# Two attentions interleaved anew, and w_hi ahead of w_lo in the 512-column ups of a two-block transformer kernel

## Chip, cores and metric

One core of one Trainium2 chip. The metric is the device time of one execution in microseconds; less is better.

## What is computed

256 tokens of width 1024 pass through two transformer blocks, all weights in float32 from HBM. First block: gated MLP mixer, convolutional FFN, **differential attention** (8 heads, two softmax maps a head, their difference times v, an RMS norm a head), the same FFN again. Second block: pooling mixer, squared-ReLU MLP, **stick-breaking attention** (16 heads; weights from log-sigmoids and reversed cumulative sums), the same MLP again. Each sublayer is `h = h + rmsnorm(sublayer(rmsnorm(h)))`.

```python
p = jax.nn.softmax(s, axis=-1); attn = p[0] - lam_full * p[1]      # differential attention
o = rmsnorm(einsum('bhqk,bhkd->bhqd', attn, v), sub_g) * (1.0 - lambda_init)
excl = lax.cumsum(log1m, axis=3, reverse=True) - log1m             # stick-breaking attention
a = jnp.where(mask, jnp.exp(jax.nn.log_sigmoid(z) + excl), 0.0)
```

## The kernel before

**Precision by splitting.** Every float32 operand is split into a rounded high part and a low remainder; a product is hi x hi + hi x lo + lo x hi, three fp32r matmuls (`three`, L592).

**Units.** The weights come as 181 units of 128 x 2048 (1 MB). For each unit SyncE loads `raw` (3 buffers; the load of u waits for w_lo of u-3, L462), ScalarE rounds it into `w_hi` (4 buffers, `split_hi`, L279), VectorE subtracts it into `w_lo` (3 buffers, `split_lo`, L288) and TensorE uses both. `unit_done` of u - 4 frees w_hi, that of u - 3 frees w_lo. Each engine's order is written out by hand, with semaphores between them; ScalarE and VectorE do their splits at fixed places among their other work (`CUT = 3` units ahead of TensorE).

**Ups of FFN and MLP** (`unit_pair`, L611): the moving operand holds the high and low half of all 256 tokens side by side. Per k-tile and output tile one matmul with w_hi over 512 columns, then one with w_lo over 256. The first three ups of a phase (`first_ups`, L677) are cut by token halves instead: `half_pair` and `low_pair` of 16 matmuls with 256 columns each.

**Downs** (`unit_down`, L720, `last_downs`, L732): 24 matmuls of 512 columns a unit, 12 a token half. At the end of FFN and MLP the last three downs run half 0 of all, then half 1; the transposes of half 0 of the next input (`turn_half`, L755) stand ahead of the last half down. Behind the attentions the last two downs do so, and the transposes follow at the end (`by_threes` is false there, L353).

**Junctions** (L1126, L1458): result -> squares (ScalarE) -> gain and residual (VectorE) -> squares -> normed input -> transposes (TensorE) -> high part (ScalarE) -> low part (VectorE), a token half at a time. `n` counts junctions: J_DIFF and J_STICK stand behind the attentions.

**Differential attention** (TensorE L941 to L957, ScalarE L1335, VectorE L1758, POOL L531). Twelve projection units, q, k, v for each of four rounds of two heads (q and k: `unit_feat`; v: `unit_token`; 48 matmuls of 256 columns each), then four downs. A round: q of j, transposes and outputs of the heads of j-1 (`diff_turn`, `diff_av`), k, transposes back of the normed heads (`diff_back`), v, scores of j. Between them ScalarE does exponentials, copies and squares; POOL makes 1/rms of four (head, token half) pairs in five small operations (L538 to L546); VectorE scales (`diff_norm`) and splits (`diff_o_lo`). Scores of head h wait for o_lo of head h-2 (L860), whose PSUM bank they take.

**Stick-breaking attention** (L1069 to L1095): ten steps (`stick_step`: scores of t, cumulative sums of t-1, outputs of t-2), placed behind certain projection units (`STICK_AT`, L77).

**POOL** runs its list in order: after the differential attention it loads gains once the second half of the next input is there (L495), builds the band matrices of the pooling mixer (L553 to L580), and only then multiplies gate and up of the second FFN (L582, `gate_up`, L329).

## Time and profile before

| | us |
|---|---|
| median of 3 runs (lowest, highest) | 1113.28 (1112.42, 1113.76) |
| the profiled execution | 1113.68 |
| its span, first to last instruction | 1111.7 |
| TensorE busy in the span | 1076.2 |
| VectorE, ScalarE, POOL busy | 756.8, 634.1, 129.1 |

Mean granted TensorE clock 0.994. Busy times are unions of the intervals in which an instruction ran. A matmul's own duration holds its way through the array, so that the distance of two starts, and not the duration, says how fast they follow each other. A row's "idle before" is the time since the engine's previous instruction ended, with what ended it.

### The profile page before, as it was taken

The numbers are of one execution on the slowest core, as the hardware profiler recorded it, in microseconds if no ns is written. First come the engines' busy times: TensorE is split into PE (matmuls) and PEld (weight loads), VectorE is DVE, ScalarE is ACT, GpSimd is POOL, SyncE is SP. The second block draws the span as 40 slices with busy tenths as digits, with TensorE's granted clock in tenths as the row PEclk, the third lists the DMA queues.
The fourth block names the chain that finished last, engine by engine and source line by source line (L and its number), as shares of the span: only waits on it lengthen the run. The fifth ranks groups of instructions, "written<-read, shape, count | busy, mean of one in ns | idle before, by whom it ended". The sixth has DMA issues, their size and how long they took to land.

```text
span 1111.7 us, 15698 instructions
## 1 busy us (share of the span) xinstructions
PE 1076.2 (97%) x6390; PEld 940.0 (85%) x6390; DVE 756.8 (68%) x883; ACT 634.1 (57%) x848; POOL 129.1 (12%) x131
## 2 busy tenths in 40 slices
PE   9999999999899988999998999999999998999997
PEld 8978888887899887888887888888899878888886
DVE  6878777667777677767668865656775657665654
ACT  6656755656655666755656544444577865453532
POOL 0001332120021155222110000000000000000000
PEclk9999999999999999999999999999999999999999
DMA  9836775454544365555552655555364234646451
GB/s 340 318 115 230 243 246 198 180 190 152 190 136 157 126 227 170 190 190 194 185 188 83 227 195 198 181 198 183 120 228 142 97 108 166 209 171 208 170 189 38
DMA packets 31142, 202.21 MB, mean 182 GB/s; under 512 B 3640, under 2 KB 3808, under 8 KB 8544
## 3 DMA queue, kind: packets, MB, share of 16 engines
q1 hardware_dynamic: 28032, 189.16, 48.3%
q0 software_dynamic: 3040, 12.07, 3.4%
q8 instruction: 50, 0.82, 0.3%
q14 instruction: 20, 0.16, 0.0%
HBM read 200.15 MB, written 2.63 MB: 182 GB/s over the span
## 4 chain that ended last, share of the span: by engine, by line
PE 75%; DVE 12%; ACT 5%; POOL 4%; issue 4%; DMA 0%; SPq 0%; DVEq 0%; ACTq 0%; POOLq 0%
PE wk L620 20%; PE wk L622 10%; PE acc L594 9%; PE acc L596 8%; PE acc L595 8%; PE wk L594 3%; PE wk L596 3%; PE wk L595 3%; DVE w_lo L295 3%; PE wk L643 2%; PE wk L652 2%; ACT w_hi L286 2%; DVE x L1477 1%; DVE region L1685 1%; PE acc L643 1%
## 5 line engine op out<-in xcount | busy, mean ns | idle before, releaser
L295 DVE TENSOR_TENSOR w_lo<-raw,w_hi 128x2048 fp32r<-128x2048 f32 x168 | 384.6, 2293 | 74.4 <-ACT w_hi L286 66.6
L620 PE MATMUL wk<-a_hl,w_hi 128*128 128x512 f32 x1024 | 363.7, 399 | 3.4 <-DVE region L1675 3.2
L286 ACT ACTIVATE w_hi<-raw 128x2048 fp32r<-128x2048 f32 x173 | 329.3, 1906 | 6.9 <-DMA raw<-ws 6.2
L622 PE MATMUL wk<-a_hl,w_lo 128*128 128x256 f32 x1024 | 287.3, 281 | 0.0
L620 PEld LDWEIGHTS wk<-a_hl,w_hi 128*128 128x128 f32 x1024 | 192.4, 188 | 51.9 <-DVE region L1675 5.0
L622 PEld LDWEIGHTS wk<-a_hl,w_lo 128*128 128x128 f32 x1024 | 193.3, 189 | 1.5
L594 PE MATMUL acc<-w_hi,b_hl 128*128 128x512 f32 x432 | 169.4, 392 | 1.3 <-DVE w_lo L295 1.3
L595 PE MATMUL acc<-w_lo,b_hl 128*128 128x512 f32 x432 | 168.5, 390 | 0.0
L596 PE MATMUL acc<-w_hi,b_hl 128*128 128x512 f32 x432 | 168.4, 390 | 0.0
L1368 ACT ACTIVATE region<-wk 128x512 f32<-128x512 f32 x30 | 17.9, 597 | 163.9 <-PE wk L622 156.7
L594 PEld LDWEIGHTS acc<-w_hi,b_hl 128*128 128x128 f32 x432 | 81.1, 188 | 19.5 <-DVE w_lo L295 2.1
L596 PEld LDWEIGHTS acc<-w_hi,b_hl 128*128 128x128 f32 x432 | 81.1, 188 | 17.7
L595 PEld LDWEIGHTS acc<-w_lo,b_hl 128*128 128x128 f32 x432 | 81.1, 188 | 15.4
L1685 DVE SCALAR_TENSOR_TENSOR region<-region,prm 128x256 f32<-128x256 f32 x176 | 78.8, 489 | 19.4 <-ACT region L1280 17.8
L1792 DVE TENSOR_TENSOR region<-wk,region 128x512 f32<-128x512 f32 x30 | 20.7, 691 | 94.3 <-ACT region L1368 94.3
L1270 ACT ACTIVATE region<-wk 128x512 f32<-128x512 f32 x42 | 24.9, 592 | 80.0 <-PE wk L622 76.3
L336 POOL TENSOR_TENSOR region<-region 128x512 f32<-128x512 f32 x20 | 49.5, 2474 | 178.4 <-ACT region L1287 178.4
L498 POOL DMA_DIRECT2D gain<-gains x13 | 7.3, 563 | 458.5 <-DVE region L1493 448.7
L594 PE MATMUL wk<-a_hl,w_hi 128*128 128x256 f32 x208 | 59.7, 287 | 0.2 <-DVE w_lo L295 0.2
L596 PE MATMUL wk<-a_hl,w_lo 128*128 128x256 f32 x208 | 58.9, 283 | 0.0
L595 PE MATMUL wk<-a_hl,w_hi 128*128 128x256 f32 x208 | 58.8, 283 | 0.0
L1675 DVE TENSOR_TENSOR region<-wk,region 128x512 f32<-128x512 f32 x42 | 28.8, 687 | 39.8 <-ACT region L1270 39.7
(256 smaller groups left out, 1658.2 us busy)
## 6 DMA issues: line engine op xcount, KB each, us to landing
raw<-ws SPq DMA_DIRECT2D x173, 1024.0 KB, 4.9
gain<-gains POOLq DMA_DIRECT2D x13, 512.0 KB, 5.0
raw<-ws SPq DMA_DIRECT2D x8, 256.0 KB, 6.6
region<-rows SPq DMA_DIRECT2D x1, 1664.0 KB, 9.6
lines_dram<-line_dram POOLq DMA_DIRECT2D x1, 1536.0 KB, 8.3
bias<-gains POOLq DMA_DIRECT2D x3, 512.0 KB, 7.0
region<-xT SPq DMA_DIRECT2D x4, 256.0 KB, 5.0
x<-x_rows SPq DMA_DIRECT2D x1, 1024.0 KB, 7.2
```

Of the source, the lines that this page charges most:

```text
L286: act.activation(w_hi[:, u % HIGH, :], raw[:, u % RAW, :], ACT.Copy).then_inc(hi_ready, 1)
L295: dve.tensor_tensor(w_lo[:, u % LOW, :], raw[:, u % RAW, :], w_hi[:, u % HIGH, :].bitcast(F32), ALU.subtract).then_inc(lo_ready, 1)
L336: eng.tensor_tensor(hf[:, p:p + 2, :], gl[:, p:p + 2, :], cv[:, p:p + 2, 1, :], ALU.mult)\
L594: pe.matmul(o, still, moving, start=first, stop=False, skip_group_check=True)
L595: pe.matmul(o, still, moving_lo, start=False, stop=False, skip_group_check=True)
L596: return pe.matmul(o, still_lo, moving, start=False, stop=last, skip_group_check=True)
L620: pe.matmul(banks[:, m, :], wh[:, k, c], a_hl[:, k, :, :].rearrange("p e t -> p (e t)"), start=k == 0, stop=False, skip_group_check=True)
L622: mm = pe.matmul(banks[:, m, T:2 * T], wl[:, k, c], a_hi[:, k, :], start=False, stop=k == DT - 1, skip_group_check=True)
L643: pe.matmul(banks[:, m, :].rearrange("p (e t) -> p e t", e=2)[:, :, c], wh[:, k, m * P:(m + 1) * P], x[:, k, :, c], start=h == 0 and k == ...
L1270: act.activation(ffn_low[:, a, :, :], ffn_banks(n, i, a)[:, :, T:2 * T], ACT.Copy).then_inc(s["low"], 1)
L1675: dve.tensor_tensor(hb[:, p + a, :, 2:HW], ffn_banks(n, i, a)[:, :, 0:T], ffn_low[:, a, :, :], ALU.add)\
L1685: dve.scalar_tensor_tensor(out=cv[:, p + a, q, :], in0=hb[:, p + a, q, tap:tap + T], scalar=prm[:, bass.ds(col, 1)], in1=cv[:, p + a, q, : ...
```

## The change

- `unit_pair` runs its 16 w_hi matmuls first, waiting for w_hi alone, and then the 16 w_lo ones (`low_pair`).
- `feat_part` and `token_part` are `unit_feat` and `unit_token` in pieces: over some k-tiles, and for v over one token half. Both attentions place scores, transposes and outputs inside units.
- Differential attention: in round 0 head 0's scores stand ahead of v's low part, head 1's in the middle of q of round 1. From round 1 on: q, transposes of both heads, 2 k-tiles of k, outputs, the rest of k, half the k-tiles of v's token half 0, transposes back, the other half, scores, v's token half 1. Mean and eps move from POOL to VectorE (`diff_rms`); POOL does the power alone.
- Stick-breaking attention: units in the order q0 q1 k0 v0 k1 v1 q2 ..., steps in the middle of units; `stick_step` of VectorE is cut in two, with a split between.
- The four downs of both attentions run by token halves (`down_tokens`), and the transposes stand ahead of the last half down. For that the last w_lo has a buffer of its own (`SPARE`).
- In both junctions ScalarE and VectorE have the order of the FFN junctions.

The diff, cut to its core ("..." where lines are left out, indentation reduced):

```diff
+STICK_UNITS = (("q", 0), ("q", 1), ("k", 0), ("v", 0), ("k", 1), ("v", 1), ("q", 2), ("k", 2), ("v", 2), ("q", 3),
+       ("k", 3), ("v", 3))
+STICK_MID = {3: 0, 4: 1, 5: 2, 6: 3, 8: 4, 9: 5, 11: 6}
+STICK_END = {11: 7}
...
+SPARE = {U_DIFF + 15: o_lo_t[:, :, :].rearrange("p k t -> p (k t)"),
+         U_STICK + 15: b_hl[:, 0:DT // 2, :, :].rearrange("p k e t -> p (k e t)")}
+def low_of(u):
+    return SPARE[u] if u in SPARE else w_lo[:, u % LOW, :]
...
+    if u == U_STICK + 15:
+        dve.wait_ge(unit_done, U_STICK + 12)
+    elif u >= LOW and u not in SPARE:
         dve.wait_ge(unit_done, u - LOW + 1)
...
 def by_threes(n):
-    return n not in (J_DIFF, J_POOL, J_STICK)
+    return n != J_POOL
...
-        over = rden[:, :, :].rearrange("p e (n m) -> p e n m", m=2)[:, :, :, 0]
-        four = lambda t: t[:, c].rearrange("p (e n) -> p e n", e=2)
-        pool.tensor_tensor(four(o_ms), four(o_ss), over, ALU.mult).then_inc(o_mean, 1)
-        pool.wait_ge(o_mean, 4 * j + 1)
-        pool.tensor_tensor(four(o_ms), four(o_ms), over, ALU.mult).then_inc(o_mean, 1)
-        pool.wait_ge(o_mean, 4 * j + 2)
-        pool.tensor_scalar(o_ms[:, c], o_ms[:, c], 1.0 / P, EPS, ALU.mult, ALU.add).then_inc(o_mean, 1)
-        pool.wait_ge(o_mean, 4 * j + 3)
-        pool.tensor_tensor(o_rs[:, c], o_ms[:, c], minus_half[:, :], ALU.pow).then_inc(o_mean, 1)
-        pool.wait_ge(o_mean, 4 * j + 4)
-        pool.tensor_tensor(four(o_rs), four(o_rs), over, ALU.mult).then_inc(o_rms, 1)
+        pool.wait_ge(o_mean, 2 * j + 2)
+        pool.tensor_tensor(o_rs[:, c], o_ms[:, c], minus_half[:, :], ALU.pow).then_inc(o_rms, 1)
...
     def unit_pair(u, banks):
-        pe.wait_ge(lo_ready, u + 1)
+        pe.wait_ge(hi_ready, u + 1)
         wh = w_hi[:, u % HIGH, :].rearrange("p (k m) -> p k m", k=DT)
-        wl = w_lo[:, u % LOW, :].rearrange("p (k m) -> p k m", k=DT)
         for k in range(DT):
             for m in range(2):
-                c = slice(m * P, (m + 1) * P)
-                pe.matmul(banks[:, m, :], wh[:, k, c], a_hl[:, k, :, :].rearrange("p e t -> p (e t)"),
+                pe.matmul(banks[:, m, :], wh[:, k, m * P:(m + 1) * P], a_hl[:, k, :, :].rearrange("p e t -> p (e t)"),
                           start=k == 0, stop=False, skip_group_check=True)
-                mm = pe.matmul(banks[:, m, T:2 * T], wl[:, k, c], a_hi[:, k, :],
-                               start=False, stop=k == DT - 1, skip_group_check=True)
-        mm.then_inc(unit_done, 1)
+        low_pair(u, banks)
...
+    def feat_part(u, bank, ks, hi=a_hi, lo=a_lo):
+        if ks[0] == 0:
+            pe.wait_ge(lo_ready, u + 1)
+        wh = w_hi[:, u % HIGH, :].rearrange("p (k m) -> p k m", k=DT)
+        wl = w_lo[:, u % LOW, :].rearrange("p (k m) -> p k m", k=DT)
+        for k in ks:
+            for m in range(2):
+                c = slice(m * P, (m + 1) * P)
+                mm = three(wk[:, bank, m * T:(m + 1) * T], wh[:, k, c], wl[:, k, c],
+                           hi[:, k, :], lo[:, k, :], k == 0 and m == 0, k == DT - 1)
+        if ks[-1] == DT - 1:
+            mm.then_inc(unit_done, 1)
+    def token_part(u, bank, h, ks, hi, lo):
+        if h == 0 and ks[0] == 0:
+            pe.wait_ge(lo_ready, u + 1)
+        c = slice(h * P, (h + 1) * P)
+        wh = w_hi[:, u % HIGH, :].rearrange("p (k m) -> p k m", k=DT)
+        wl = w_lo[:, u % LOW, :].rearrange("p (k m) -> p k m", k=DT)
+        for k in ks:
+            mm = three(wk[:, bank, h * T:(h + 1) * T], hi[:, k, c], lo[:, k, c], wh[:, k, :], wl[:, k, :],
+                       k == 0 and h == 0, k == DT - 1)
+        if h and ks[-1] == DT - 1:
+            mm.then_inc(unit_done, 1)
...
+    def down_tokens(n, u, h, pair, res, first=False):
+        last = u == LAST[n]
+        if h == 0:
+            pe.wait_ge(lo_ready, u + 1)
+        for f in range(2):
+            for kk in range(2):
+                mm = down_half(u, h, kk, f, *pair, res, first and kk == 0, last and kk == 1)
+            if last:
+                mm.then_inc(unit_done if h and f else res_done, 1)
+        if h and not last:
+            mm.then_inc(unit_done, 1)
...
+    def diff_first(base):
+        half_pair(base, wk[:, 0:2, :], J_FFN0, 0)
+        half_pair(base + 1, wk[:, 2:4, :], J_FFN0, 0)
+        turn_half(J_FFN0, 1)
+        half_token(base + 2, acc[:, 3, :], J_FFN0, 0, a_hi, a_lo)
+        half_pair(base, wk[:, 0:2, :], J_FFN0, 1)
+        low_pair(base, wk[:, 0:2, :])
+        half_pair(base + 1, wk[:, 2:4, :], J_FFN0, 1)
+        low_pair(base + 1, wk[:, 2:4, :])
+        half_token(base + 2, acc[:, 3, :], J_FFN0, 1, a_hi, a_lo)
+        pe.wait_ge(dq_ready, 1)
+        pe.wait_ge(dk_ready, 1)
+        diff_scores(0)
+        low_token(base + 2, acc[:, 3, :], a_hi)
+        feat_part(base + 3, 0, range(0, 4))
+        pe.wait_ge(dv_ready, 2)
+        diff_scores(1)
+        feat_part(base + 3, 0, range(4, DT))
+    diff_first(U_DIFF)
     for j in range(1, 4):
-        projections(U_DIFF, j, 0, dreleased)
-        outputs_pair(j - 1)
-        projections(U_DIFF, j, 1, dreleased)
+        u = U_DIFF + 3 * j
+        if j > 1:
+            pe.wait_ge(dq_ready, j)
+            feat_part(u, 0, range(DT))
+        pe.wait_ge(dk_ready, j)
+        if j > 1:
+            pe.wait_ge(dv_ready, 2 * j)
+            diff_turn(2 * j - 2)
+            diff_turn(2 * j - 1)
+            feat_part(u + 1, 1, range(0, 2))
+            diff_av(2 * j - 2)
+            diff_av(2 * j - 1)
+            feat_part(u + 1, 1, range(2, DT))
+        else:
+            diff_turn(0)
+            feat_part(u + 1, 1, range(0, 4))
+            diff_av(0)
+            diff_turn(1)
+            feat_part(u + 1, 1, range(4, 6))
+            diff_av(1)
+            feat_part(u + 1, 1, range(6, DT))
+        pe.wait_ge(dv_ready, 2 * j)
+        token_part(u + 2, 2, 0, range(0, 4), a_hi, a_lo)
         diff_back(j - 1)
-        projections(U_DIFF, j, 2, dreleased)
-        scores_pair(j)
-    pe.wait_ge(dv_ready, 8)
-    unit_down(U_DIFF + 12, *b_pair(0), True, res=wk)
+        token_part(u + 2, 2, 0, range(4, DT), a_hi, a_lo)
+        pe.wait_ge(dq_ready, j + 1)
+        pe.wait_ge(dk_ready, j + 1)
+        diff_scores(2 * j)
+        diff_scores(2 * j + 1)
+        token_part(u + 2, 2, 1, range(DT), a_hi, a_lo)
+    u = U_DIFF + 12
+    down_tokens(J_DIFF, u, 0, b_pair(0), wk, True)
+    down_tokens(J_DIFF, u + 1, 0, b_pair(1), wk)
     outputs_pair(3)
-    unit_down(U_DIFF + 13, *b_pair(1), False, res=wk)
+    down_tokens(J_DIFF, u + 2, 0, b_pair(2), wk)
     diff_back(3)
-    last_downs(J_DIFF, U_DIFF + 14, (b_pair(2), b_pair(3)), (None, (o_lo, 8)), res=wk)
+    down_tokens(J_DIFF, u, 1, b_pair(0), wk, True)
+    pe.wait_ge(o_lo, 8)
+    down_tokens(J_DIFF, u + 3, 0, b_pair(3), wk)
+    down_tokens(J_DIFF, u + 1, 1, b_pair(1), wk)
+    down_tokens(J_DIFF, u + 2, 1, b_pair(2), wk)
+    turn_half(J_DIFF, 0)
+    down_tokens(J_DIFF, u + 3, 1, b_pair(3), wk)
     ffn_phase(1, U_FFN1, J_DIFF)
...
+        q0, q1, k0 = wk[:, 0:2, :], wk[:, 2:4, :], acc[:, 2:4, :]
+        turn_half_kv(0)
+        half_pair(base, q0, J_MLP0, 0)
+        half_pair(base + 1, q1, J_MLP0, 0)
+        pe.wait_ge(blo_ready, 2)
+        turn_half(J_MLP0, 1)
+        half_pair(base + 2, k0, J_MLP0, 0, b_hl, True)
+        half_pair(base, q0, J_MLP0, 1)
+        turn_half_kv(1)
+        low_pair(base, q0)
+        half_pair(base + 1, q1, J_MLP0, 1)
+        low_pair(base + 1, q1)
+        half_pair(base + 2, k0, J_MLP0, 1, b_hl, True)
+        low_pair(base + 2, k0, b_hi)
...
+    for c in range(3, 12):
+        if c == 3:
+            pe.wait_ge(sq_ready, 2)
+        stick_unit(c, 0)
+        if c in STICK_MID:
+            stick_there(STICK_MID[c])
+            stick_step(STICK_MID[c])
+        stick_unit(c, 1)
+        if c in STICK_END:
+            stick_there(STICK_END[c])
+            stick_step(STICK_END[c])
...
+    u = U_STICK + 12
+    pe.wait_ge(so_lo, 2)
+    down_tokens(J_STICK, u, 0, o_pair(0), wk, True)
+    pe.wait_ge(so_lo, 4)
+    down_tokens(J_STICK, u + 1, 0, o_pair(1), wk)
     pe.wait_ge(sv_ready, 8)
-    pe.wait_ge(so_lo, 2)
-    unit_down(U_STICK + 12, *o_pair(0), True, res=wk, last_bank=(so_lo, 6))
     stick_step(8)
-    unit_down(U_STICK + 13, *o_pair(1), False, res=wk)
+    pe.wait_ge(so_lo, 6)
+    down_tokens(J_STICK, u + 2, 0, o_pair(2), wk)
     stick_step(9)
-    last_downs(J_STICK, U_STICK + 14, (o_pair(2), o_pair(3)), (None, (so_lo, 8)), res=wk)
+    down_tokens(J_STICK, u, 1, o_pair(0), wk, True)
+    pe.wait_ge(so_lo, 8)
+    down_tokens(J_STICK, u + 3, 0, o_pair(3), wk)
+    down_tokens(J_STICK, u + 1, 1, o_pair(1), wk)
+    down_tokens(J_STICK, u + 2, 1, o_pair(2), wk)
+    turn_half(J_STICK, 0)
+    down_tokens(J_STICK, u + 3, 1, o_pair(3), wk)
...
-        if by_threes(n):
-            input_hi(0)
+        if n == J_MLP0:
+            split_hi(act, last + 3)
+        input_hi(0)
         result_squares(1)
-        if not by_threes(n):
-            input_hi(0)
...
-    for j in range(4):
+    low_copy(U_DIFF, wk[:, 0:2, :], diff_low[:, 0, :, :], d_low)
+    split_hi(act, U_DIFF + 3)
+    low_copy(U_DIFF + 1, wk[:, 2:4, :], diff_low[:, 1, :, :], d_low)
+    split_hi(act, U_DIFF + 4)
+    token_copy(U_DIFF + 2, 0, 3, av, ACT.Copy, dv_ready, src=acc)
+    diff_exp(0)
+    diff_exp(1)
+    diff_probs(0)
+    split_hi(act, U_DIFF + 5)
+    diff_probs(1)
+    diff_squares(0)
+    diff_squares(1)
+    for j in range(1, 4):
         u = U_DIFF + 3 * j
-        if j:
+        if j > 1:
             diff_outputs(j - 1)
-        else:
-            low_copies(u, diff_low, d_low)
         split_hi(act, u + CUT)
-        if j:
-            diff_o_hi(j - 1)
         split_hi(act, u + 1 + CUT)
-        token_copy(u + 2, j, 2 if j else 3, av, ACT.Copy, dv_ready, src=wk if j else acc)
-        split_hi(act, u + 2 + CUT)
+        diff_o_hi(j - 1)
         diff_exp(2 * j)
         diff_exp(2 * j + 1)
+        token_copy(u + 2, j, 2, av, ACT.Copy, dv_ready)
+        split_hi(act, u + 2 + CUT)
...
+    low_copy(U_STICK + 1, wk[:, 2:4, :], stick_low[:, 1, :, :], s_low)
+    act.wait_ge(sq_ready, 1)
+    low_copy(U_STICK + 2, acc[:, 2:4, :], stick_low[:, 0, :, :], s_low)
+    split_hi(act, U_STICK + 4)
+    split_hi(act, U_STICK + 5)
+    for c in range(3, 12):
+        kind, j = STICK_UNITS[c]
+        if c in STICK_MID:
+            stick_step(STICK_MID[c])
+        split_hi(act, U_STICK + c + CUT)
+        if kind == "v":
+            token_copy(U_STICK + c, j, 2, av, ACT.Copy, sv_ready)
+        if c in STICK_END:
+            stick_step(STICK_END[c])
+    split_hi(act, U_STICK + 15)
     stick_step(8)
-    split_hi(act, U_STICK + 12 + CUT)
...
-        if by_threes(n):
-            lo_half(dve, last + 1, 0)
+        lo_half(dve, last + 1, 0)
...
-            lo_half(dve, last + 1, 1)
-            input_lo(0)
+        lo_half(dve, last + 1, 1)
+        input_lo(0)
...
+    def diff_rms(j):
+        c = slice(4 * j, 4 * j + 4)
+        under = den[:, :, :].rearrange("p e (n m) -> p e n m", m=2)[:, :, :, 0]
+        four = lambda t: t[:, c].rearrange("p (e n) -> p e n", e=2)
+        dve.scalar_tensor_tensor(out=four(o_rs), in0=under, scalar=EPS, in1=under, op0=ALU.mult, op1=ALU.mult)                   .then_inc(o_mean, 1)
+        dve.wait_ge(o_mean, 2 * j + 1)
+        dve.wait_ge(o_squared, 4 * (j + 1))
+        dve.scalar_tensor_tensor(out=four(o_ms), in0=four(o_ss), scalar=1.0 / P, in1=four(o_rs), op0=ALU.mult,
+                                 op1=ALU.add).then_inc(o_mean, 1)
...
-    for j in range(4):
+    feat_sum(wk[:, 0:2, :], diff_low[:, 0, :, :], d_low, 1, qT[:, 0:2, :], dq_ready)
+    split_lo(dve, U_DIFF + 3)
+    feat_sum(wk[:, 2:4, :], diff_low[:, 1, :, :], d_low, 2, kT[:, 0:2, :], dk_ready)
+    diff_bias(0)
+    split_lo(dve, U_DIFF + 4)
+    diff_combine(0)
+    diff_bias(1)
+    diff_combine(1)
+    split_lo(dve, U_DIFF + 5)
+    for j in range(1, 4):
         u = U_DIFF + 3 * j
-        if j == 0:
-            feat_sum(u, 0, diff_low, d_low, qT[:, 0:2, :], dq_ready)
-            feat_sum(u + 1, 1, diff_low, d_low, kT[:, 0:2, :], dk_ready)
-        else:
-            feat_copy(u, 0, qT[:, 2 * j:2 * j + 2, :], dq_ready)
-        split_lo(dve, u + CUT)
-        if j:
-            diff_norm(j - 1)
-            feat_copy(u + 1, 1, kT[:, 2 * j:2 * j + 2, :], dk_ready)
-            diff_o_lo(j - 1)
-        split_lo(dve, u + 1 + CUT)
+        feat_copy(u, 0, qT[:, 2 * j:2 * j + 2, :], dq_ready)
+        if j == 1:
+            split_lo(dve, u + CUT)
+        diff_rms(j - 1)
+        diff_norm(j - 1)
+        if j > 1:
+            split_lo(dve, u + CUT)
+        feat_copy(u + 1, 1, kT[:, 2 * j:2 * j + 2, :], dk_ready)
+        if j > 1:
+            split_lo(dve, u + 1 + CUT)
+        diff_o_lo(j - 1)
         for part in (diff_bias, diff_combine):
             part(2 * j)
             part(2 * j + 1)
+        if j == 1:
+            split_lo(dve, u + 1 + CUT)
         split_lo(dve, u + 2 + CUT)
+    diff_rms(3)
+    diff_norm(3)
     split_lo(dve, U_DIFF + 12 + CUT)
-    diff_norm(3)
     diff_o_lo(3)
-    split_lo(dve, U_DIFF + 13 + CUT)
     junction(J_DIFF)
...
+    feat_sum(wk[:, 0:2, :], stick_low[:, 0, :, :], s_low, 1, qT[:, 0:2, :], sq_ready)
+    split_lo(dve, U_STICK + 3)
+    feat_sum(wk[:, 2:4, :], stick_low[:, 1, :, :], s_low, 2, qT[:, 2:4, :], sq_ready)
+    feat_sum(acc[:, 2:4, :], stick_low[:, 0, :, :], s_low, 3, kT[:, 0:2, :], sk_ready)
+    for c in range(3, 12):
+        kind, j = STICK_UNITS[c]
         u = U_STICK + c
-        if c == 0:
-            feat_sum(u, 0, stick_low, s_low, qT[:, 0:2, :], sq_ready)
-            feat_sum(u + 1, 1, stick_low, s_low, kT[:, 0:2, :], sk_ready)
-        elif kind == 0:
+        if c in STICK_MID:
+            stick_weights(STICK_MID[c])
+        if c == 3:
+            split_lo(dve, U_STICK + 4)
+        split_lo(dve, u - 1 + CUT)
+        if kind == "q":
             feat_copy(u, 0, qT[:, 2 * j:2 * j + 2, :], sq_ready)
-        elif kind == 1 and j:
+        elif kind == "k":
             feat_copy(u, 1, kT[:, 2 * j:2 * j + 2, :], sk_ready)
-        if c in STICK_AT:
-            stick_step(STICK_AT[c], split=u + CUT)
-        else:
-            split_lo(dve, u + CUT)
-    stick_step(8)
+        if c in STICK_MID:
+            stick_rest(STICK_MID[c])
+    stick_weights(7)
+    split_lo(dve, U_STICK + 11 + CUT)
+    stick_rest(7)
+    stick_weights(8)
+    stick_rest(8)
     split_lo(dve, U_STICK + 12 + CUT)
-    stick_step(9)
-    split_lo(dve, U_STICK + 13 + CUT)
+    stick_weights(9)
```

## Rows read from the trace of the kernel before

**Rows 1.** The profile page of the kernel before, parts 1 and 4.
```profile
PE 1076.2 (97%) x6390; PEld 940.0 (85%) x6390; DVE 756.8 (68%) x883; ACT 634.1 (57%) x848; POOL 129.1 (12%) x131
...
PE 75%; DVE 12%; ACT 5%; POOL 4%; issue 4%; DMA 0%; SPq 0%; DVEq 0%; ACTq 0%; POOLq 0%
```

**Rows 2.** Waits of TensorE: total us, times, longest us.
```profile
PE wk L643 <- DVE a_hl L1500: 7.3, 2, 3.7
...
PE acc L875 <- DVE region L1732: 3.4, 4, 1.4
...
PE acc L863 <- ACT region L1207: 1.0, 1, 1.0
```

**Rows 3.** The page's group of the 512-column ups, and its timeline over one unit.
```profile
L620 PE MATMUL wk<-a_hl,w_hi 128*128 128x512 f32 x1024 | 363.7, 399 | 3.4 <-DVE region L1675 3.2
...
461.44 0.40 PE L620 MATMUL wk<-a_hl,w_hi 128*128 128x512 f32 x1
...
467.09 0.40 PE L594 MATMUL acc<-w_hi,b_hl 128*128 128x512 f32 x1
```

**Rows 4.** Timeline of a run of 512-column and of one of 256-column matmuls.
```profile
450.29 0.40 PE L594 MATMUL acc<-w_hi,b_hl 128*128 128x512 f32 x1
...
451.47 0.39 PE L596 MATMUL acc<-w_hi,b_hl 128*128 128x512 f32 x1
...
455.80 0.39 PE L620 MATMUL wk<-a_hl,w_hi 128*128 128x512 f32 x1
...
621.00 2.08 PE L652 MATMUL wk<-a_hl,w_lo 128*128 128x256 f32 x16
622.92 2.08 PE L643 MATMUL wk<-a_hl,w_hi 128*128 128x256 f32 x16
```

**Rows 5.** Windows: from:to, length, busy us (count) of each engine, PEclk, DMA share, GB/s.
```profile
274.94:280.19 5.25, 4.00 (x33) 3.78 (x31) 3.61 (x9) 3.70 (x9) 0.00 (x0) 1.00 0.38 158
393.15:403.80 10.65, 6.83 (x42) 6.26 (x42) 6.55 (x14) 6.93 (x14) 2.55 (x5) 0.84 0.10 33
920.32:930.67 10.35, 6.67 (x41) 6.22 (x41) 6.28 (x13) 6.66 (x14) 0.53 (x1) 0.84 0.11 34
...
925.20:928.61 3.41, 3.30 (x15) 3.33 (x16) 2.20 (x5) 2.21 (x4) 0.46 (x1) 0.50 0.00 0
...
814.52:920.32 105.80, 104.71 (x755) 93.43 (x753) 63.59 (x62) 80.72 (x91) 0.00 (x0) 1.00 0.40 140
```

**Rows 6.** One round of the first attention: its window, then rows of the timeline.
```profile
319.74:342.52 22.78, 22.14 (x184) 21.28 (x183) 16.38 (x27) 12.97 (x33) 3.79 (x5) 1.00 0.41 140
...
328.25 0.55 PE L875 MATMUL acc<-ident,region 128*128 128x128 f32 x3 [0.56 <-DVE region L1732]
...
329.93 0.39 PE L887 MATMUL acc<-region 128*128 128x128 f32 x2
...
330.87 1.92 ACT L286 ACTIVATE w_hi<-raw 128x2048 fp32r<-128x2048 f32 x1
331.06 0.20 POOL L538 TENSOR_TENSOR o_ms<-o_ss,region 128x4 f32<-128x4 f32 x1 [18.65 <-ACT region L1318]
...
331.90 1.01 POOL L544 TENSOR_TENSOR o_rs<-o_ms,minus_half 128x4 f32<-128x4 f32 x1
332.81 2.29 DVE L295 TENSOR_TENSOR w_lo<-raw,w_hi 128x2048 fp32r<-128x2048 f32 x1 [1.81 <-ACT w_hi L286]
```

**Rows 7.** Timeline: the norm of round 1, and the transposes that wait for it.
```profile
312.44 1.13 DVE L1741 TENSOR_SCALAR region<-acc,o_rs 128x128 f32<-128x128 f32 x4
...
313.15 0.91 PE L896 MATMUL acc<-ident,region 128*128 128x128 f32 x4
```

**Rows 8.** The chain of waits after the first attention: start us, us, what.
```profile
400.96 0.29 issue
...
426.64 1.26 POOL region L336
...
438.89 0.50 PE wk L620
```

167 lines of the change are left out of this document (60 added, 107 removed).

## The prediction

> **What bounds the kernel now.** I read the page first. TensorE is busy 97% of the span and makes 75% of the chain that ends last [rows 1]; VectorE and ScalarE stand at 68% and 57%. So only two things can move the time: how closely TensorE's matmuls follow one another, and the 35 us in which it stands idle, or runs at half clock. The view of its waits [rows 2] says where it idles: 7.3 us in two pauses of up to 3.7 us at the junctions behind the two attentions, 3.4 us in the first attention (transposes of the probabilities wait for VectorE), 1.0 us there at the first scores; and 3.2 us at the 512-column ups [rows 3], at the start of the second FFN. Then I went into these places one by one.
>
> **Part 1: the order inside a 512-column up.** Before, each w_hi matmul (512 columns) is followed by its w_lo one (256 columns). One unit of 16 such pairs starts at 461.44 and is over at 467.09: 5.65 us [rows 3]. The page counts 1024 pairs, thus 64 units. The change runs 16 w_hi, then 16 w_lo. What the two kinds cost in runs of their own is in [rows 4]: 24 matmuls of 512 columns take 450.29 to 455.80; its first 5 take 1.18 us (0.236 each), the other 19 take 4.33 (0.228 each). 16 matmuls of 256 columns take 622.92 - 621.00 = 1.92 us. If the wide run is slow at its start each time, a unit costs 1.18 + 11 x 0.228 + 1.92 = 5.61; if it isn't, 16 x 0.228 + 1.92 = 5.57. That is 0.04 to 0.08 us a unit, 2.6 to 5.1 us over 64. I take **4.0**, between, since the rows show a slow start behind alternating matmuls and none behind a run of narrow ones. About 0.3 is lost where TensorE waits for others afterwards (second FFN's start). So **-3.7**. The wait for w_lo moves behind the w_hi run; no row of TensorE in these lines waits for w_lo, so that gives nothing. The bound against me: a wide run that stays at 0.236 and w_lo as now gives 5.70, +3 us over 64.
>
> By the Trainium skill ("TensorE: Matmul & The Clock Gate", Back-to-back issue gap) the distance of two matmuls follows from the column count alone, so that an order of the same matmuls would be worth 0. The trace does not agree fully: the pair takes 0.353 alternating, 0.348 in runs.
>
> **Part 2: junctions behind the attentions.** Today the last two downs alone are run by token halves, and the transposes of half 0 come after all downs. In the first FFN's junction, whose order the attentions are now given (transposes of half 0 before the last down's half 1), TensorE reaches the transposes of half 1 5.25 us after the last down, at full clock; in the attentions' junctions it takes 10.65 and 10.35 us, with a mean clock of 0.84 [rows 5]. The clock fell to 0.50 (1.2 GHz) for 3.41 us just when TensorE resumed from its pause [rows 5]; half of that, 1.7 us, is lost. The 1.4 us pause of the first FFN's junction had no such fall. After the change the way is 1.3 us (8 transposes, now ahead of the last half down) + 0.3 us (their wait) + 5.25 = 6.9. For the second attention: 10.35 - 6.9 = **-3.4**. Nothing behind it waits for something else: TensorE has no wait in the last MLP. Bounds: -1.7 (the clock still falls) to -4.
>
> **Part 3: the second attention's body.** Same matmuls, eight steps of scores, sums and outputs as before, put inside value and query projections in place of between them. In this stretch TensorE has work for 104.7 of 105.8 us and ScalarE, the next, for 80.7 [rows 5], so a step's chain on ScalarE and VectorE is covered, in either order. About 1 us of TensorE's idle time there may go, and I count as much anew (the first value unit waits for the second q sum; the last two cumulative sums wait for ScalarE, which gets a split between step 7 and step 8). **0**, bounds -1.5 to +2.
>
> **Part 4: the first attention's body.** One round takes 22.78 us now [rows 6], 48 x 3 projections' matmuls at 0.12 us making 17.3 of it. What goes: the scores' wait for ScalarE (1.0 idle) and the transposes' waits (3.4 idle, four of them) [rows 2]. These are idle times from one matmul's end to the next one's start; in starts, as the wait of [rows 6] at 328.25 shows (0.56 idle, 0.76 later than the two transposes' own distance), each costs 0.2 more: 1.0 + 3.4 + 5 x 0.2 = 5.4. The waits for the norm, too short for a row, are estimated at 0.2 to 0.3 each, together 0.9: about 6.3 us. POOL's chain of five small operations (331.06 to the norm at about 335.2) shrinks to the power alone (1.01).
>
> What comes: VectorE's order in round 1 is copy q, *split of unit 6*, then the mean, the power (POOL), the norm. That split needs ScalarE's w_hi of unit 6, which stands behind both heads' squares. From the last output matmul (329.93) to the squares' end (331.06) is 1.1 us; + ScalarE's split 1.9, VectorE's split 2.3 (its row waits for just this split of ScalarE now, 1.81 us), two small operations 0.4 (as L538, 0.20 each), the power 1.1, first norm to transposes 0.7 (312.44 to 313.15, [rows 7]) = 7.5 us. TensorE has as cover two k-tiles of the k unit (12 matmuls, 1.44) and a quarter of the v unit (12, 1.44). So it waits about 7.5 - 2.9 - 0.2 = **4.4 us**; now the whole k unit (5.8) covers 5.9.
> Rounds 2 and 3: scores of a round need o_lo, which VectorE does behind norm, split, copy and split: 1.1 + 0.4 + 1.1 + 1.1 + 2.3 + 0.7 + 2.3 + 0.5 = 9.5 us behind the last output matmul; TensorE's cover is 36 + 12 + 12 matmuls and the transposes, 7.2 + 0.7, and gaps: wait 1.2 each, **2.4**. The end (norm 3, o_lo 8, turn) 0.9. Four more changes between f32 and f32r matmuls and the short blocks, 0.2 each: 0.8. Sum: 4.4 + 2.4 + 0.9 + 0.8 - 6.3 = +2.2.
>
> The junction: half 1's normed input is there at 400.96 [rows 8], 7.8 us behind the last down (393.15). New: 1.6 + 5.25 + 0.7 = 7.5. That is -0.3. **All that counts here is this moment**, since POOL builds the bands only then: the chain of waits runs from 400.96 through POOL to 426.64 (its first gate of the FFN) and leaves it only near 438.89, where TensorE resumes [rows 8]. Whatever TensorE gains at this junction, its clock too, ends in a longer wait at 430 to 439. So +1.9 stays whole. A pause of 4.4 us is longer than the 3.7 us behind which the clock fell; the same fall costs up to 1.7, part of it may lie in the pause itself: I take 1.3; and 0.2 for one more fall at the longer wait in the FFN. First attention: **+3.4**, bounds -0.5 (VectorE's split finds its w_hi earlier than I count, no fall) to +6.
>
> The skill's same page (HAM oscillation) says that idle gaps bring the clock down to half; by it the fall behind the 4.4 us wait is sure, and the two falls at the junctions go. The trace agrees in that each pause of 3.7 us had one.
>
> **Sum.** -3.7 - 3.4 + 0 + 3.4 = **-3.7 us**. The profiled execution took 1113.68 (span 1111.7 and 2.0 around it), 0.4 above the median 1113.28; I put the change against the median: 1109.6.
>
> **Rivals.**
> A. *The first attention loses nothing* (the waits at the norm are covered, and the clock stays): -3.7 - 3.4 + 0 = 1106.2. For it: VectorE is busy only 16.4 of 22.8 us in a round, POOL's chain gets 3 us shorter. Against: the order of round 1 leaves 2.9 us of cover. 20%.
> B. *The order of the ups gives nothing*, as the rule above has it: 0 - 3.4 + 3.4 = 1113.3. For it: the slow start of the wide run. 13%.
> C. *The pause behind the second attention stays long enough for the clock to fall*: -3.7 - 1.7 + 3.4 = 1111.3. Against: the same order at the first FFN pauses 1.4 us. 10%.
> D. *Slower: wide runs never settle.* Each change from 256 to 512 columns shows 0.236 to 0.24 for five matmuls. If a run across two banks stays at 0.240, a unit costs 16 x 0.240 + 1.92 = 5.76, +0.11, and 64 units +7.0: 1113.3 + 7.0 = 1120.3. It passes into slower from a mean of 0.236 on (with parts 2 to 4 at 0, +0.03 us a unit = 2.2 us). Against: 19 of 24 run at 0.228, though in one bank's groups. 8%.
> My forecast has the rest, 49%.
>
> **Numbers.** 0.2% (2.2 us) is about what a measurement of this kernel can tell. The forecast with its bounds is faster in four of five of its cases; with A that makes 0.65 faster; B, C and the forecast's upper end 0.27 same; 0.08 slower. The range goes from 1105.0 (below A) to 1113.9 (above B), leaving out D and the tails.
>
> **What would show it.** L620's block of 16 in 3.65 to 3.75 us and L652's in 1.92; two falls of the clock fewer at the junctions, the transposes of half 1 5.25 us after the last down; a TensorE wait of 4 us or so for L1741's kind (norm) in round 1 with a fall of the clock right behind; o_lo ending waits of about 1 us ahead of the scores in rounds 2 and 3; POOL's bands starting 2 to 3.5 us later, and the waits at the second FFN's start longer than 3.2 us. I am wrong if the norm's wait in round 1 is under 2 us, if blocks of w_hi take 3.8 us or more, or if the second attention shows new waits of over 2 us in total.

## The result and the profile after

The changed kernel takes 1102.66 us (median of 4 runs, 1102.10 to 1103.36) beside 1113.50 for the kernel before in the same session: ratio 0.9904, 95% interval 0.9892 to 0.9915, so 10.8 us less. The forecast was 1109.6, its range 1105.0 to 1113.9: the direction was right, the gain almost three times what was forecast, and the time outside the range. The profiled execution took 1102.57, its span 1100.7 (before 1113.68 and 1111.7).

The page of the changed kernel, parts 1, 4 and 5:

```profile
PE 1066.9 (97%) x6390; PEld 939.1 (85%) x6390; DVE 757.6 (69%) x893; ACT 634.5 (58%) x849; POOL 115.8 (11%) x115
...
PE 77%; DVE 12%; issue 4%; ACT 4%; POOL 3%; DMA 1%; SPq 0%; DVEq 0%; ACTq 0%; POOLq 0%
...
L619 PE MATMUL wk<-a_hl,w_hi 128*128 128x512 f32 x1024 | 243.8, 390 | 4.5 <-DVE region L1781 4.4
```

The same matmuls, the same engine ahead. Its waits, from the view of TensorE's waits (total us, times, longest):

```profile
PE wk L619 <- DVE region L1781: 4.4, 4, 2.7
PE acc L921 <- DVE region L1859: 4.1, 1, 4.1
PE acc L888 <- DVE b_hl L1865: 2.2, 2, 1.1
```

The two pauses of 3.7 us of [rows 2] are gone, and so is the 3.4 us for VectorE in the first attention. New are a wait of 4.1 us for the norm (L921) and two for o_lo (L888), both forecast; and the ups at the second FFN's start wait 4.2 of these 4.4 us (the rest is in the first FFN), not 3.2.

To see where the 11.0 us of span went, I took marks that both traces have, mostly the start of `turn_half(n, 1)`, the transposes of half 1 at each junction:

| mark | before | after | shift | of this stage |
|---|---|---|---|---|
| GMLP's junction | 89.72 | 89.38 | -0.34 | -0.34 |
| first FFN's junction | 280.19 | 278.22 | -1.97 | -1.63 |
| last wait at the second FFN's start over | 438.89 | 436.85 | -2.04 | **-0.07** |
| second FFN's junction | 597.92 | 594.24 | -3.68 | -1.64 |
| first 512-column up of MLP 0 | 630.60 | 626.16 | -4.44 | **-0.76** |
| first MLP's junction | 799.07 | 793.12 | -5.95 | -1.51 |
| first 512-column up of MLP 1 | 944.98 | 935.32 | -9.66 | **-3.71** |
| end of the span | 1111.7 | 1100.7 | -11.0 | -1.34 |

The four rows of stages full of 512-column ups give 1.63 + 1.64 + 1.51 + 1.34 = 6.1. The second attention with its junction gives 3.7, the first attention 0.1, a junction that the change does not touch 0.8, and 0.3 was there before the first 512-column up (in the runs below the mark of the GMLP's junction lies between 89.05 and 90.14).

**The ups.** Timeline of the changed kernel over two units and the down behind them:

```profile
453.55 3.79 PE L619 MATMUL wk<-a_hl,w_hi 128*128 128x512 f32 x16
457.18 2.08 PE L649 MATMUL wk<-a_hl,w_lo 128*128 128x256 f32 x16
459.09 3.82 PE L619 MATMUL wk<-a_hl,w_hi 128*128 128x512 f32 x16
462.75 2.08 PE L649 MATMUL wk<-a_hl,w_lo 128*128 128x256 f32 x16
464.66 0.40 PE L595 MATMUL acc<-w_hi,b_hl 128*128 128x512 f32 x1
```

By the starts, 16 w_hi take 3.63 and 3.66, 16 w_lo 1.91. Two units take 11.11 us; the same two before:

```profile
472.59 0.39 PE L620 MATMUL wk<-a_hl,w_hi 128*128 128x512 f32 x1
...
483.88 0.40 PE L594 MATMUL acc<-w_hi,b_hl 128*128 128x512 f32 x1
...
472.59:489.38 16.79, 16.79 (x89) 1.00 0.54 188
```

11.29 us; with the down behind them 16.79 against 16.58 (453.55 to 470.13). So 0.09 us a unit, and the down takes 5.47 in place of 5.50, so 0.03 more. In the MLPs, one up and its down have a period of 11.01 (637.20 to 648.21) in place of 11.11 (641.76 to 652.87 before). That is 0.10 a unit with its share of the down in either phase, 6.4 over 64 units; a little of it is lost in the first ups of a phase.

**The junction behind the second attention.** Windows of the changed kernel, from the transposes of half 0 and from the end of the last down to the transposes of half 1:

```profile
911.60:920.74 9.14, 7.88 (x52) 6.96 (x52) 6.99 (x14) 6.28 (x14) 0.00 (x0) 1.00 0.35 115
915.49:920.74 5.25, 3.99 (x33) 3.78 (x31) 3.61 (x9) 3.70 (x9) 0.00 (x0) 1.00 0.38 158
```

The 5.25 us are those of [rows 5] to the hundredth, at full clock. The 0.31 us wait and the 1.07 us of transposes ahead of the last down make 6.63, where it was 10.35.

**The first attention.** Timeline of round 1, VectorE and TensorE:

```profile
309.61 2.29 DVE L308 TENSOR_TENSOR w_lo<-raw,w_hi 128x2048 fp32r<-128x2048 f32 x1 [2.58 <-ACT w_hi L297]
313.40 1.13 DVE L1859 TENSOR_SCALAR region<-acc,o_rs 128x128 f32<-128x128 f32 x4 [1.23 <-POOL o_rs L547]
314.06 1.21 PE L921 MATMUL acc<-ident,region 128*128 128x128 f32 x4 [4.08 <-DVE region L1859]
...
313.00:319.80 6.80, 5.74 (x28) 5.13 (x30) 3.01 (x8) 0.95 (x2) 0.36 (x1) 0.50 0.41 146
```

TensorE waits as forecast, and the clock is at 0.50 (1.2 GHz) for 6.8 us, 5.7 of them behind the wait, where I had priced a stretch of 3.4. And still this attention cost nothing in the end. The timeline of POOL, first of the kernel before, then of the changed one, has the reason (the last row of each is VectorE's, its three splits):

```profile
401.25 1.17 POOL L498 DMA_DIRECT2D gain<-gains  x2 [20.55 <-DVE region L1493]
405.55 8.62 POOL L563 TENSOR_SCALAR_AFFINE_SELECT region<-region 128x256 f32<-128x256 f32 x8
...
426.61 1.28 POOL L336 TENSOR_TENSOR region<-region 128x512 f32<-128x512 f32 x1
...
406.27 7.13 DVE L295 TENSOR_TENSOR w_lo<-raw,w_hi 128x2048 fp32r<-128x2048 f32 x3
```

```profile
401.58 1.12 POOL L511 DMA_DIRECT2D gain<-gains  x2 [22.86 <-DVE region L1603]
405.84 6.29 POOL L564 TENSOR_SCALAR_AFFINE_SELECT region<-region 128x256 f32<-128x256 f32 x8
...
424.57 1.29 POOL L349 TENSOR_TENSOR region<-region 128x512 f32<-128x512 f32 x1
...
403.27 6.88 DVE L308 TENSOR_TENSOR w_lo<-raw,w_hi 128x2048 fp32r<-128x2048 f32 x3
```

POOL starts 0.33 us later than before, 2.3 later against the first FFN's end, but its first gate comes 2.04 us earlier. Eight affine selects take 8.62 or 6.29 us: one takes 0.3 to 0.4 by itself and 2.2 to 2.4 where a split of VectorE runs beside it, and three met one before, two after. Shortest, median and longest of the eight in ns, before and changed:

```profile
L563 POOL TENSOR_SCALAR_AFFINE_SELECT region<-region x8: 293/403/2445, 405.5 to 413.9; 128x256 f32<-128x256 f32 x4, 128x128 f32<-128x128 f32 x4
L564 POOL TENSOR_SCALAR_AFFINE_SELECT region<-region x8: 288/394/2327, 405.8 to 411.8; 128x256 f32<-128x256 f32 x4, 128x128 f32<-128x128 f32 x4
```

The one fewer is the 2.3 us. By the Trainium skill ("SBUF — State Buffer", SBUF: two separate sides) VectorE and GpSimd share a port pair that whichever starts first holds for its whole instruction while the other is blocked, where both read SBUF and VectorE has two inputs there; the trace agrees: each of the five long affine selects ends 0.1 to 0.3 us behind the split beside it. VectorE's three splits stand behind the a_lo of half 1, thus behind TensorE's transposes of half 1, and these come 3.1 us earlier (403.80, 400.68).

### The profile page after: what moved, and what is told of

Same layout as the page of the kernel before. It is cut to its first block, busy times and chain, and to the rows that moved or that the text cites. A ratio compares the mean times of both kernels' runs of the same rounds, so it can differ in the third digit from the quotient of the medians.

```text
span 1100.7 us, 15695 instructions
## 1 busy us (share of the span) xinstructions
PE 1066.9 (97%) x6390; PEld 939.1 (85%) x6390; DVE 757.6 (69%) x893; ACT 634.5 (58%) x849; POOL 115.8 (11%) x115
## 4 chain that ended last, share of the span: by engine, by line
PE 77%; DVE 12%; issue 4%; ACT 4%; POOL 3%; DMA 1%; SPq 0%; DVEq 0%; ACTq 0%; POOLq 0%
PE wk L619 19%; PE wk L649 11%; PE acc L595 8%; PE acc L596 8%; PE acc L597 8%; PE wk L595 4%; PE wk L597 4%; PE wk L596 4%; DVE w_lo L308 4%; PE wk L640 1%; DVE x L1587 1%; DVE region L1603 1%; DVE region L1791 1%; DVE w_lo L319 1%; PE acc L640 1%
## 5 line engine op out<-in xcount | busy, mean ns | idle before, releaser
L308 DVE TENSOR_TENSOR w_lo<-raw,w_hi 128x2048 fp32r<-128x2048 f32 x164 | 375.0, 2290 | 60.8 <-ACT w_hi L297 53.6
L619 PE MATMUL wk<-a_hl,w_hi 128*128 128x512 f32 x1024 | 243.8, 390 | 4.5 <-DVE region L1781 4.4
L649 PEld LDWEIGHTS wk<-a_hl,w_lo 128*128 128x128 f32 x1216 | 155.1, 191 | 5.1
L649 PE MATMUL wk<-a_hl,w_lo 128*128 128x256 f32 x1216 | 158.0, 283 | 0.0
L595 PE MATMUL wk<-a_hl,w_hi 128*128 128x256 f32 x192 | 55.2, 288 | 0.0
L597 PE MATMUL wk<-a_hl,w_lo 128*128 128x256 f32 x192 | 54.3, 283 | 0.0
L596 PE MATMUL wk<-a_hl,w_hi 128*128 128x256 f32 x192 | 54.3, 283 | 0.0
```

What stands on the lines that cost most here:

```text
L308: dve.tensor_tensor(low_of(u), raw[:, u % RAW, :], w_hi[:, u % HIGH, :].bitcast(F32), ALU.subtract).then_inc(lo_ready, 1)
L595: pe.matmul(o, still, moving, start=first, stop=False, skip_group_check=True)
L596: pe.matmul(o, still, moving_lo, start=False, stop=False, skip_group_check=True)
L597: return pe.matmul(o, still_lo, moving, start=False, stop=last, skip_group_check=True)
L619: pe.matmul(banks[:, m, :], wh[:, k, m * P:(m + 1) * P], a_hl[:, k, :, :].rearrange("p e t -> p (e t)"), start=k == 0, stop=False, skip_gr ...
L649: mm = pe.matmul(banks[:, m, T:2 * T], wl[:, k, m * P:(m + 1) * P], hi[:, k, :], start=False, stop=k == DT - 1, skip_group_check=True)
```

## Experiments

Times of the runs are held against 1113.5 to 1113.8 for the kernel before, measured with each group of runs. Intervals are at 95%.

**1. The ups' order alone.** The kernel before, with

```diff
-                pe.wait_ge(lo_ready, u + 1)
+                pe.wait_ge(hi_ready, u + 1)
...
-                        mm = pe.matmul(banks[:, m, T:2 * T], wl[:, k, c], a_hi[:, k, :],
-                                       start=False, stop=k == DT - 1, skip_group_check=True)
-                mm.then_inc(unit_done, 1)
+                low_pair(u, banks)
```

> The kernel before with one part of the change alone: a 512-column up runs its 16 w_hi matmuls, then its 16 w_lo ones. Theory S (the units' closer spacing is the largest part of the gain; in the changed kernel's trace a unit takes 5.545 us where it took 5.65): 64 x 0.10 = 6.4 us, 0.3 to 1 of it lost where the second FFN's start waits for POOL's gate: -5.5 to -6.3 us, about 1107.5. Rival P (the prediction's own size, 0.04 to 0.08 us a unit): -2.3 to -4.8, about 1109.6. Rival N (the order alone gives nothing, the shift comes from the attentions): within 1 us of before. A fall of TensorE's clock at a junction that comes or goes is worth up to 1.7 us either way and is read in the granted clock.

1107.51 us, ratio 0.9948 (0.9934 to 0.9963): -6.2 us. Theory S holds, P and N fall. That alone is 1.7 times what the prediction gave the part. By the marks of its trace the four stages of ups give 6.0 of the 6.0 us of span. The rest cancels: the clock did not fall at the pooling junction (-0.8), but it stood at half for 6.8 us, not 3.4, behind the pause at the second attention (+0.7).

**2. Everything but the ups' order.** The changed kernel with the old `unit_pair`.

> The changed kernel with its 512-column ups alternating again, all else of the change kept. Theory S: the change less 6 us, so 4.5 to 5.3 us faster than before (about 1108.5). Rival P: the change less 4, so 6.5 to 7 us faster (1106.7). Rival N: as the changed kernel, 10.8 us faster (1102.7).

1109.96 us, ratio 0.9966 (0.9954 to 0.9977): -3.7 us, +7.3 on the changed kernel. That is beyond what S had named (-4.5 to -5.3), on the side away from P and N. What S left out is the pooling junction: here the clock fell behind it as before, in the changed kernel it did not (0.8 us, below). The four stages of ups take what they took before, to 0.14 us in all. This run prices the attentions without the ups. Its marks are 280.71 (+0.52 on before), 439.06 (+0.17) and, for the first 512-column up of MLP 1, 941.95 (-3.03), with 799.21 (+0.14) ahead: the first attention gives -0.35, the second -3.2. It shows the failed step in its plainest form, as nothing but the attentions differs from before:

```profile
403.83 1.12 POOL L511 DMA_DIRECT2D gain<-gains  x2 [22.86 <-DVE region L1607]
408.08 6.30 POOL L564 TENSOR_SCALAR_AFFINE_SELECT region<-region 128x256 f32<-128x256 f32 x8
...
426.78 1.28 POOL L349 TENSOR_TENSOR region<-region 128x512 f32<-128x512 f32 x1
```

POOL starts at 403.83, against 401.25: less the 0.52 this is 2.06 us later, close to the +1.9 that I had worked out. The gate comes at 426.78 against 426.61, 0.35 earlier by the same measure.

**3, 4. What in the order of the ups costs.** First groups of two (`for m in range(2)` around each kind), then strict alternation with each w_lo matmul one step later, so that its bank isn't that of the matmul ahead.

> The changed kernel with ups in groups of two w_hi and two w_lo matmuls: half as many changes between 512 and 256 columns as alternating, no wide run longer than two. Theory S1 (each change of width costs, 0.0065 us a pair of changes): half of the gain stays, 3 us slower than the changed kernel, 1105.8. Theory S2 (the first five wide matmuls behind a narrow one are slow, 0.236 in place of 0.227): nothing stays, 6 us slower, 1108.7. Theory S3 (what costs is that w_lo's result bank is that of the matmul just ahead, which groups of two avoid): all stays, 1102.7.

> The changed kernel with ups that alternate between 512 and 256 columns, but each w_lo matmul one w_hi matmul later than before, so that it never adds into the bank of the matmul just ahead of it. Theory S3 (what cost 0.1 us a unit was that bank): all of the gain stays, 1102.7 to 1103.5. Rival S4 (the alternation itself costs it): nothing stays, 6 to 7 us slower than the changed kernel, 1109.5.

Groups of two: 1103.50, ratio 0.9910 (0.9895 to 0.9924). Crossed alternation: 1109.18, ratio 0.9956 (0.9942 to 0.9970). The windows over two units and their down, of groups of two, then of the crossed order:

```profile
454.09:470.68 16.59, 16.59 (x90) 1.00 0.58 192
```

```profile
455.34:472.09 16.75, 16.75 (x90) 1.00 0.55 190
```

16.79 alternating, 16.75 crossed, 16.59 by twos, 16.58 in runs. Groups of two also keep the old wait for w_lo ahead of the unit, so that the moved wait is worth at most the 0.8 us by which they are slower than the changed kernel. The bank is worth little (S3 falls with the second run); a single narrow matmul between wide ones costs (S4), and two together are nearly as good as sixteen, which neither S1 nor S2 had. Why two suffice stays open.

**5. The wait for the norm in round 1.** The changed kernel with

```diff
-                if j == 1:
-                    split_lo(dve, u + CUT)
                 diff_rms(j - 1)
                 diff_norm(j - 1)
-                if j > 1:
-                    split_lo(dve, u + CUT)
+                split_lo(dve, u + CUT)
```

> The changed kernel with VectorE's order in round 1 of the first attention turned: mean, norm, and only then the split of unit 6, as in rounds 2 and 3. Theory W (the 4.2 us wait for the norm and the 5.8 us at half clock behind it, worth 2.9, are real time, and what is gained before the second FFN is kept): 4.0 + 2.9 less a new wait of about 1.5 us for o_lo ahead of the round's scores: 5.4 us faster than the changed kernel, 1097.3. Rival K (the start of the second FFN waits for POOL anyway, as the prediction's part 4 has it for what TensorE gains): under 1 us faster, 1102.

1098.87 us, ratio 0.9868 (0.9853 to 0.9883): 3.8 less than the changed kernel, where W had 5.4. The profiled execution took 1097.99 at a mean clock of 0.999, 4.6 less than the changed kernel's; two of the four took 1099.8 and 1099.9, at 0.996. TensorE's waits in the first attention are now

```profile
PE acc L888 <- DVE b_hl L1865: 3.6, 3, 1.4
PE acc L785 <- DVE region L1603: 1.4, 2, 1.3
```

The wait for the norm is gone, a third one for o_lo came (1.4), and in this execution the clock does not fall before the span's end. The transposes of half 1 behind this attention stand 117.50 us behind the first FFN's (122.46 in the changed kernel): 5.0 us. The last wait at the second FFN's start is over at 432.19, 4.66 earlier. So K falls: what TensorE gains here is kept.

**6. POOL started later.** The changed kernel with four more memsets ahead of the bands.

> The changed kernel with four more memsets (1.4 us with their wait) on POOL ahead of the bands. Theory V (POOL's progress there is pinned to the end of VectorE's three splits, beside which one of POOL's operations takes 2.2 us in place of 0.4; the 1.4 us are swallowed by the first of them): POOL's first gate and the time as in the changed kernel, 1102.7. Rival C (the chain runs from the normed input through POOL at fixed length, as the prediction's part 4 had it): gate and second FFN's start 1.4 us later, 1104.1.

1102.48 us, ratio 0.9900 (0.9886 to 0.9915). The timeline of POOL:

```profile
401.10 1.12 POOL L512 DMA_DIRECT2D gain<-gains  x2 [22.91 <-DVE region L1607]
...
405.35 1.50 POOL L560 MEMSET region<- 128x384 f32 x4
406.93 4.74 POOL L568 TENSOR_SCALAR_AFFINE_SELECT region<-region 128x256 f32<-128x256 f32 x8
...
424.11 1.28 POOL L350 TENSOR_TENSOR region<-region 128x512 f32<-128x512 f32 x1
```

From its start to its gate POOL takes 23.01 us; in the changed kernel, with 1.5 us less to do, 22.99. C, the prediction's reading, falls. V holds in that the time and the gate stay; what sets the length is how many of POOL's operations meet a split (one of the eight here, two in the changed kernel), not a fixed distance from the last split.

**7, 8. What removed the pause behind the second attention.** The changed kernel with `turn_half(J_STICK, 0)` one line further down, behind the last down's half 1; and the kernel before with the order of transposes alone:

```diff
-            return n not in (J_DIFF, J_POOL, J_STICK)
+            return n != J_POOL
```

(and without VectorE's two splits `U_DIFF + 13 + CUT` and `U_STICK + 13 + CUT`, which `lo_half` now does).

> The changed kernel with the transposes of half 0 of the second attention's junction behind the last down's half 1. Theory J (their place is what took the pause away): VectorE's a_lo of half 0 comes 2.8 us later and the results of half 1 wait behind it; the transposes of half 1 come 1 to 1.5 us later than in the changed kernel, and 2.5 to 3 us with a fall of the clock: 1104 to 1105.6. Rival Q (the four downs by token halves are what helps, the order of the transposes is worth nothing): 1102.7.

> The kernel before with the order of the first FFN's junction given to the junctions behind both attentions (transposes of half 0 ahead of the last down's half 1; VectorE's split of the next unit in halves), and nothing else of the change. Behind the second attention both theories expect the way from the downs' end to the transposes of half 1 to fall from 10.35 to about 6.7 us (-3.6). Behind the first attention the normed input of half 1 comes only 0.3 to 0.5 us earlier, but TensorE's transposes of it, and with them VectorE's three splits, about 3 us earlier. Theory V (POOL's bands end 2.3 us behind the last of VectorE's three splits, not at a fixed time behind the normed input): the second FFN starts 2.0 to 2.5 us earlier, in all -5.6 to -6.1 us, 1107.6. Rival C (POOL's chain has a fixed length from the normed input, as the prediction's part 4 had it): the second FFN starts 0.3 to 0.5 us earlier, in all -4 us, 1109.5.

Late transposes: 1103.42, ratio 0.9909 (0.9894 to 0.9924), 0.8 above the changed kernel, between Q and the least that J had named (1104, so 1.3). The time alone can't part them, as in its profiled execution the clock also fell behind the pooling junction; the marks can. The order alone: 1116.17, ratio 1.0021 (1.0012 to 1.0031), slower than before, where both theories expected a gain. The timelines, first of the late transposes, then of the order alone behind the first attention:

```profile
914.66 1.03 PE L785 MATMUL acc<-ident,region 128*128 128x128 f32 x8
916.77 4.07 PE L640 MATMUL wk<-a_hl,w_hi 128*128 128x256 f32 x32 [1.07 <-DVE a_hl L1610]
922.11 1.32 PE L785 MATMUL acc<-ident,region 128*128 128x128 f32 x8 [1.28 <-DVE region L1603]
```

```profile
393.15 1.32 PE L760 MATMUL acc<-ident,region 128*128 128x128 f32 x8 [2.88 <-DVE region L1493]
403.91 0.33 PE L760 MATMUL acc<-ident,region 128*128 128x128 f32 x1 [1.26 <-DVE region L1493]
```

With late transposes the way from the downs' end to half 1 is 7.45 us, 0.8 above the change's 6.63; 2.9 of the 3.7 stay. Q is nearer than J. With the order alone TensorE stands 2.9 us ahead of the transposes of half 0, since one half down (12 matmuls, 2.7 us) is all that runs between half 0's sums and those transposes; in the change two run there, and TensorE waits 0.3. So the four downs by halves pay for most of the junction, and the early transposes, with only two downs by halves, just move the pause ahead. The first FFN's junction, my model for the new length, has three units by halves and thus two half downs at that place; the prediction took its 5.25 us over without naming this. No run has the four downs by halves with the old order of ScalarE and VectorE, so what that order adds by itself stays open.

This run was also to tell V from C, and with the gain gone it can't do it as planned. But POOL starts 3.56 us later in it than before (404.81) and gates only 1.27 later (427.88), with the same transposes of half 1 as before (403.91): once more the chain behind POOL's start is not of fixed length (23.07 us from start to gate, 25.36 before; two affine selects are long here, three before).

**9, 10. The second FFN's start.** The changed kernel with the bands built ahead of POOL's wait for the junction:

```diff
+            pool.wait_ge(attn_turned, 8)
-            load_gains(J_FFN1)
-            for which, r in enumerate((2 * J_POOL, 2 * J_POOL + 1, ROW_POOL_SCALE)):
-                pool.dma_start(late[:, which, :], gains[r:r + 1, :].broadcast_to([P, D])).then_inc(late_landed, 16)
```

with those loads behind the bands; and then with them behind the second gate (`if i == 1:` in the loop over `gate_up`).

> The changed kernel with POOL's eight bands built as soon as head 7's probabilities are transposed (about 383 us) in place of behind the junction's normed input (402 to 425 us). Theory G (the start of the second FFN waits for POOL's first gate, which stands behind the bands): its waits for VectorE, 4.7 us in starts, fall to the 0.6 us of the first FFN's start: 4.0 us faster than the changed kernel, 1098.7. Rival H (VectorE's own queue of splits sets that start): under 1 us faster, 1102.

> The run with early bands once more, now also with POOL's five loads of 512 KB (two gains, three rows for the pooling) behind its second gate in place of ahead of its first. Theory D (there the wait for POOL was followed by the landing of a weight unit, 8.5 us from issue where the median is 4.9, since these loads ran beside it): the wait of 2.0 us at the third up goes, the start of the second FFN is 1.5 to 2 us earlier than with early bands alone, and no fall of the clock behind it (another 0 to 1.6): 1099.5 to 1100.5. Rival E (the unit's landing is late because its buffer comes free late): as with early bands alone, 1102.6.

Early bands: 1102.61, ratio 0.9906 (0.9890 to 0.9923), nothing gained. Loads later too: 1099.30, ratio 0.9876 (0.9859 to 0.9892), 3.4 less. Early bands alone, the chain of waits and TensorE's waits at the FFN's start; then with the loads later:

```profile
406.24 8.47 DMA raw<-ws
414.74 1.93 ACT w_hi L297
416.69 2.29 DVE w_lo L308
...
PE wk L617 <- DVE region L1779: 1.9, 1, 1.9
```

```profile
PE wk L618 <- DVE region L1780: 0.2, 1, 0.2
```

Theory G was right that POOL ends the wait and wrong that nothing stood close behind it: a weight unit took 8.5 us to land beside POOL's 2.5 MB of loads. It held an up for 1.9 us, and the clock fell for 3.4 us behind it. With the loads out of the way both are gone (D, and E falls). That fall is not tied to the bands: behind the 2.7 us wait of the same up it came in experiments 6 and 7 too, and not in the changed kernel.

**11. A better version.** The edits of 5 and 10, and `diff_o_lo` ahead of the second split in rounds 2 and 3.

> The changed kernel with what the runs so far point to: the norm ahead of the split in round 1 of the first attention (measured: -3.8 us), o_lo ahead of the second split in rounds 2 and 3 (the round's scores wait 1.27 us for it in each of three rounds: -3.8), early bands with POOL's loads behind its second gate (0 to -3). Expected: 1102.7 - 3.8 - 3.8 - 2 = 1093 if these add up; 1095 if the second FFN's start keeps its waits; 1098.9 if the time of o_lo only moves to the next wait.

1093.44 us, ratio 0.9819 (0.9805 to 0.9834), 9.2 less than the changed kernel, as forecast, but not by the forecast's terms. Experiments 5 and 10 had measured 3.8 and 3.4, which leaves 2.0 for the order of o_lo, where 3.8 stood. Its waits in rounds 2 and 3 are gone (1.1 us each in the view of waits), that of round 1 stays (1.4). The order of o_lo was not run by itself.

## Why the prediction was wrong

- **Part 1, -3.7: undersized; measured -6.2.** The mechanism was right. In its step "5.61 ... 5.57" a unit was to take 0.04 to 0.08 us less; it takes 0.09 less, and the down behind two units 0.03 less, which no term had. I had charged every wide run with half of the slow start of [rows 4] (0.04 us); a run behind a down shows none of it (3.63), one behind a narrow run 0.03 (3.66). Rival B is refuted by experiment 1. By the Trainium skill ("TensorE: Matmul & The Clock Gate", Back-to-back issue gap) an order of the same matmuls is worth 0. No run here bears that out; experiment 1 measured 6.2 us.
- **Part 2, -3.4: right**, 10.35 to 6.63 for 6.9 forecast (the transposes take 1.07, not 1.3), with the fall of the clock gone. The reason was only half named (experiments 7 and 8).
- **Part 3, 0: right.** From the transposes of half 1 at the first MLP's junction to the downs' end, less the 1.38 us ahead of the last down, it is 120.99 us, 121.25 before.
- **Part 4, +3.4: wrong; measured -0.1, and -0.35 without the ups' change.** Its body was nearly right: wait 4.1 to 4.2 for the norm (4.4 forecast), twice 1.27 by the starts for o_lo (twice 1.2 forecast), POOL's start 2.06 us later (1.9). The clock's fall was twice as long as the one priced at 1.3, so that other terms were probably somewhat too high; the runs don't part them. What failed is the next sentence: "All that counts here is this moment, since POOL builds the bands only then", and that TensorE's gain at the junction "ends in a longer wait". POOL's start is no fixed distance from its gate. VectorE's splits end earlier when TensorE's transposes of half 1 come earlier, fewer of POOL's operations meet one, and that gives back 2.3 us (experiment 2; 6 and 8 show the mechanism). The waits at the second FFN's start did grow, from 3.2 to 4.2 us, but behind transposes that came 3.1 us earlier.
- **No term at all: -0.8** at the pooling junction. This part is luck, neither the change's work nor foreseen: it has the same code and the same 2.1 us wait in both kernels. Before, the clock fell behind it at 614.6, a third fall that the prediction had not seen (42 matmuls from the transposes on took 6.40 us), after it did not (5.64):

```profile
614.77:621.17 6.40, 6.40 (x42) 6.40 (x43) 6.20 (x5) 3.00 (x3) 0.53 (x1) 0.75 0.56 193
```

```profile
611.08:616.72 5.64, 5.40 (x42) 4.96 (x43) 5.64 (x5) 3.00 (x3) 0.53 (x1) 1.00 0.53 173
```

- The sum: -3.7 became -0.3 - 6.1 - 0.1 - 0.8 - 3.7 = -11.0. The range's lower end let part 4 fall to zero with parts 1 and 2 at their middle values; part 1 then came out beyond its own bound of 5.1, and the clock added its share. The chances were also added up wrongly: four fifths of 49% with A make 0.59 faster, not 0.65, and B, C and the rest of the forecast 0.33, not 0.27.
